# Two transformer blocks on one core: another order and another split of work in the attention pairs, and an output written in parts

## The reference

```python
# differential attention (4 head pairs): two softmaxes over the same values
p = softmax(q k^T * HD**-0.5)                  # one for each of the two maps
w = p[:, :, 0] - lam * p[:, :, 1]; out = w @ v # v is 128 wide
# windowed attention with sinks, neighbourhood attention, MLA: per head
out = softmax(q k^T * scale + bias) @ v        # v is 64 wide
# lam = exp(sum(lq1*lk1)) - exp(sum(lq2*lk2)) + lam_init
x = x + 0.5 * mx[8] * swiglu(...)              # the last layer's result is the output
```

## Time and profile before

| | |
|---|---|
| Median of 3 runs | 2604.9 us (2600.58 to 2605.96) |
| The profiled execution's own time | 2598.19 us |
| Its span | 2596.4 us |
| PE busy | 2490.1 us (96%), weight loads 2157.3 us (83%) |
| DVE busy | 1350.2 us (52%) |
| ACT busy | 1035.2 us (40%) |

### The profile page before, as it was taken

The page is one execution under the profiler, slowest core; times in us unless marked ns, Lnnn a source line. Parts: engine busy times, 40 slices in busy tenths (PEclk is TensorE's granted clock), DMA queues, the critical chain, the costliest instruction groups (busy, mean ns, idle before and its releaser), DMA issues.

```text
span 2596.4 us, 37247 instructions
## 1 busy us (share of the span) xinstructions
PE 2490.1 (96%) x15710; PEld 2157.3 (83%) x15710; DVE 1350.2 (52%) x2245; ACT 1035.2 (40%) x1659; POOL 0.2 (0%) x4
## 2 busy tenths in 40 slices
PE   7999999999999999999789999999999999988998
PEld 6998789978997888888568888888888887868998
DVE  6657554655453334357886333335333347846554
ACT  5534544434433223146563322213222226744442
POOL 0000000000000000000000000000000000000000
PEclk9999999999999999999999999999999999999999
DMA  9886733488862333335102323332333326502554
GB/s 334 283 277 207 234 122 98 145 321 302 311 211 90 97 98 98 97 122 186 41 1 66 103 96 96 96 97 90 97 97 97 98 89 181 184 1 67 185 180 137
DMA packets 145639, 372.28 MB, mean 143 GB/s; under 512 B 20266, under 2 KB 65730, under 8 KB 145474
## 3 DMA queue, kind: packets, MB, share of 16 engines
q1 hardware_dynamic: 145186, 369.59, 44.0%
q10 hardware_dynamic: 288, 0.31, 0.1%
HBM read 368.71 MB, written 1.15 MB: 142 GB/s over the span
## 4 chain that ended last, share of the span: by engine, by line
PE 88%; DVE 7%; ACT 3%; issue 1%; DMA 1%; SPq 0%; ACTq 0%; DVEq 0%
PE psum L352 76%; PE psum L834 2%; PE psum L1701 2%; PE psum L1672 1%; DVE normed_raw L618 1%; DVE normed_lo L631 1%; PE psum L1689 1%; PE psum L1603 1%; PE psum L1291 1%; PE psum L1303 1%; DVE weights_lo L300 1%; DVE arena L1768 0%; ACT arena L1721 0%; PE psum L1166 0%; PE psum L1275 0%
## 5 line engine op out<-in xcount | busy, mean ns | idle before, releaser
L300 DVE TENSOR_TENSOR weights_lo<-weights_raw,weights_hi 128x1024 fp32r<-128x1024 f32 (+2 forms) x547 | 656.9, 1212 | 471.8 <-ACT weights_hi L294 469.0
L352 PE MATMUL psum<-normed_hi,weights_hi 128*128 128x256 f32 (+2 forms) x2664 | 880.6, 331 | 21.6 <-DVE normed_lo L631 6.8
L352 PE MATMUL psum<-normed_lo,weights_hi 128*128 128x256 f32 (+2 forms) x2664 | 866.7, 325 | 0.0
L352 PE MATMUL psum<-normed_hi,weights_lo 128*128 128x256 f32 (+2 forms) x2664 | 866.3, 325 | 0.0
L294 ACT CAST weights_hi<-weights_raw 128x1024 fp32r<-128x1024 f32 (+2 forms) x547 | 562.8, 1035 | 371.8 <-DMA weights_raw<-in_w_down 260.9
L352 PEld LDWEIGHTS psum<-normed_hi,weights_hi 128*128 128x128 f32 (+1 forms) x2664 | 508.6, 191 | 85.5 <-issue 35.1
L352 PEld LDWEIGHTS psum<-normed_lo,weights_hi 128*128 128x128 f32 (+1 forms) x2664 | 509.8, 191 | 41.5 <-issue 1.2
L352 PEld LDWEIGHTS psum<-normed_hi,weights_lo 128*128 128x128 f32 (+1 forms) x2664 | 509.6, 191 | 40.6
L352 PE MATMUL psum<-hidden_hi,weights_hi 128*128 128x512 f32 (+1 forms) x594 | 217.6, 366 | 0.0
L352 PE MATMUL psum<-hidden_hi,weights_lo 128*128 128x512 f32 (+1 forms) x594 | 217.1, 365 | 0.0
L352 PE MATMUL psum<-hidden_lo,weights_hi 128*128 128x512 f32 (+1 forms) x594 | 217.1, 365 | 0.0
(11 more groups left out here) (264 smaller groups left out, 2740.3 us busy)
## 6 DMA issues: line engine op xcount, KB each, us to landing
weights_raw<-in_w_gu SPq DMA_DIRECT2D x220, 512.0 KB, 3.6
weights_raw<-in_w_down SPq DMA_DIRECT2D x110, 512.0 KB, 3.6
arena<-in_w_mod SPq DMA_DIRECT2D x72, 512.0 KB, 6.9
weights_raw<-in_w_x SPq DMA_DIRECT2D x24, 512.0 KB, 6.5
resid<-in_w_mod SPq DMA_DIRECT2D x24, 512.0 KB, 7.5
normed_raw<-in_w_mod SPq DMA_DIRECT2D x24, 512.0 KB, 7.9
under_normed_hi<-in_w_mod SPq DMA_DIRECT2D x24, 512.0 KB, 7.7
weights_raw<-in_w_qk SPq DMA_DIRECT2D x24, 512.0 KB, 4.3
```

The lines of the kernel that those rows point to most:

```text
L300: ve.tensor_tensor(w_lo[:, c % RING, a], w_raw[:, c % RING, a], w_hi[:, c % RING, a].bitcast(F32), ALU.subtract).then_inc(lo_ready, 1)
L352: last = te.matmul(out, a, b, start=start and n == 0, stop=stop and n == 2)
```

## The change

Five things change.

1. In `Attend`, PE now does the value products of unit i-3 ahead of the transposes of unit i-2. ACT copies banks 4 and 5 with one instruction; DVE's copy (L1735) and its semaphore go.
2. In a difference, L1779 goes. The second map's factor is formed as -lambda times the ratio of the sums, and one operation joins the maps; a second reciprocal comes behind it, and the output is scaled where it was copied. Other units scale both outputs with one operation instead of two.
3. In the second pass the side steps move: the second normalisation goes behind step 1, the eight turns behind steps 2 to 5.
4. `Modulation` waits for the constants only from its first transposes on.
5. The meetings of the engines, `Turn` and `Store` go. `Output` writes the result in five parts, woven into the last `IntoResid`, which no longer sums squares: four transposes each behind steps 7, 12 and 18 of its 22, and two transposes twice behind the last.

```diff
-                if 2 <= i < len(self.units) + 2:          # PE: transposes of unit i-2
-                    ...
                 if i >= 3:                                 # PE: values of unit i-3
                     j, u = i - 3, self.units[i - 3]
                     pe.wait_ge(aa_copied, self.base + j + 1)
-                    pe.wait_ge(*u.second)
                     ...
+                if 2 <= i < len(self.units) + 2:
+                    j, u = i - 2, self.units[i - 2]
+                    pe.wait_ge(*u.probs)
+                    if j >= 1:
+                        pe.wait_ge(aa_copied, self.base + j)
+                    ...
+                    last.then_inc(aa_turned, 1)
@@ Attend.scalar
-                    w = len(u.values[0]) * P
-                    se.copy(self.turned[:, j % 2, 0, 0:w], psum[:, 4, 0:w]).then_inc(aa_copied, 1)
+                    n, w = len(u.values), len(u.values[0]) * P
+                    se.copy(self.turned[:, j % 2, 0:n, 0:w], psum[:, 4:4 + n, 0:w]).then_inc(aa_copied, 1)
@@ Attend.vector
-                        ve.tensor_copy(self.turned[:, j % 2, 1, 0:w], psum[:, 5, 0:w]).then_inc(aa_copied2, 1)
...
+                    if u.lam is not None:
+                        last = ve.tensor_scalar(u.out, sums, stat[:, 2:3], None, ALU.mult)
+                    else:
+                        each = stat[:, 2:4].rearrange("p (n o) -> p n o", o=1).to_broadcast([P, 2, HD])
+                        last = ve.tensor_tensor(u.out, sums.rearrange("p (n d) -> p n d", n=2), each, ALU.mult)
@@ Attend.weights
-                step(ve.reciprocal(stat[:, 2:4], stat[:, 2:4]))
-                step(ve.tensor_tensor(stat[:, 3:4], stat[:, 3:4], u.lam, ALU.mult))
-                step(ve.tensor_scalar(s[:, 1, 0:u.width], s[:, 1, 0:u.width], stat[:, 3:4], None, ALU.mult))
+                step(ve.reciprocal(stat[:, 3:4], stat[:, 3:4]))
+                step(ve.scalar_tensor_tensor(out=stat[:, 3:4], in0=stat[:, 3:4], scalar=stat[:, 2:3], in1=u.lam,
+                                             op0=ALU.mult, op1=ALU.mult))
+                ve.scalar_tensor_tensor(out=s[:, 0, 0:u.width], in0=s[:, 1, 0:u.width], scalar=stat[:, 3:4],
+                                        in1=s[:, 0, 0:u.width], op0=ALU.mult, op1=ALU.add).then_inc(aa_probs, 1)
+                step(ve.reciprocal(stat[:, 2:3], stat[:, 2:3]))
@@ Modulation.tensor
                     pe.wait_ge(cond_in, 1)
+                elif k < 0:
                     pe.wait_ge(const_in, 32)
-                elif k < 0:
                     pe.wait_ge(mod_rows, r)
@@ second pass
-        side = [(0, h_steps[24]), (0, h_steps[25])]
-        side += [(1 + n // 2, t_steps[18 + n]) for n in range(8)]
+        side = [(0, h_steps[24]), (1, h_steps[25])]
+        side += [(2 + n // 2, t_steps[18 + n]) for n in range(8)]
@@ output
+            parts = ((0, 2), (2, 4), (4, 6), (6, 7), (7, 8))
+            def tensor(self, pe, i):
+                a, b = self.parts[i]
+                pe.wait_ge(*bank_free[self.down.group + b - 1])
+                for t in range(NT):
+                    for k in range(a, b):
+                        last = te.transpose(self.turned(i)[:, t, (k - a) * P:(k - a + 1) * P],
+                                            resid[:, k, t * P:(t + 1) * P], ident)
+                last.then_inc(out_mm, 1)
+            def scalar(self, act, step, i):
+                a, b = self.parts[i]
+                act.wait_ge(out_mm, i + 1)
+                se.copy(result[:, :, a * P:b * P], self.turned(i)).then_inc(out_copied, 1)
+            def sync(self, sp, i):
+                a, b = self.parts[i]
+                sp.wait_ge(out_copied, i + 1)
+                sp.dma_start(out[0].rearrange("(t p) n -> p t n", p=P)[:, :, a * P:b * P],
+                             result[:, :, a * P:b * P]).then_inc(out_done, 16)
...
-        alone(*chain, norm, *ffn(W["w_gu21"], W["w_down21"], KF, TOK, hidden_x, (1, 8), [norm]))
-        alone(Turn(...)); segments.append(([([Store()], 0, 1)], 0))
+        up, down = ffn(W["w_gu21"], W["w_down21"], KF, TOK, hidden_x, (1, 8), [norm], sums=False)
+        side = [((b * KF - 1) // CT + 2, step) for (_, b), step in zip(Output.parts, output)]
+        in_order(steps_of(*chain, norm, up), beside(steps_of(down), side))
```

More of the change, by code:

```diff
@@ L1680, in tensor @@
                     last.then_inc(aa_scores, 1)
-                if 2 <= i < len(self.units) + 2:
-                    j, u = i - 2, self.units[i - 2]
-                    pe.wait_ge(*u.probs)
-                    if j >= 1:
-                        pe.wait_ge(aa_copied, self.base + j)
-                        pe.wait_ge(*self.units[j - 1].second)
-                    for n in range(len(u.values)):
-                        for k in range(len(u.values[n])):
-                            last = te.transpose(psum[:, 4 + n, k * P:(k + 1) * P],
-                                                self.s[:, j % 3, n, k * P:(k + 1) * P], ident)
-                    last.then_inc(aa_turned, 1)
                 if i >= 3:
@@ L1704, in tensor @@
                     last.then_inc(aa_pv, 1)
+                if 2 <= i < len(self.units) + 2:
[3 more added lines that the diff above has]
+                        pe.wait_ge(aa_copied, self.base + j)
+                    for n in range(len(u.values)):
+                        for k in range(len(u.values[n])):
+                            last = te.transpose(psum[:, 4 + n, k * P:(k + 1) * P],
+                                                self.s[:, j % 3, n, k * P:(k + 1) * P], ident)
+                    last.then_inc(aa_turned, 1)
             def scalar(self, act, step, i):
@@ L1986, in ffn @@
+        def ffn(up, down, tiles, a, pair, gate, norms, tail=None, sums=True):
             first = FfnUp(up, tiles, a, pair, norms)
-            second = IntoResid(down, tiles, pair[1:], slice(0, a.stop - a.start), gate, tail=tail)
+            second = IntoResid(down, tiles, pair[1:], slice(0, a.stop - a.start), gate, sums=sums, tail=tail)
             second.ready = first.hidden_ready
@@ L2018, in build @@
         ctx_norm.have = lambda k: [(ctx_in, 16)]
-        segments.append(([
+        segments.append([
             ([attn_branch, mixer_out, norm2, *ffn0], 0, 1),
@@ L2023, in build @@
             ([Modulation(1, mod_ring1, (a1_max, NT * HG))], 0.1, 0.95),
-        ], 0))
+        ])
         last_norm = Norm(TOK, lambda k, s: col("final", k), None, into=resid)
-        def alone(*stages):
-            segments.append(([([stage], 0, 1) for stage in [Merged(steps_of(*stages))]], 1))
         def in_order(*lists):
-            segments.append(([([Merged([step for steps in lists for step in steps])], 0, 1)], 0))
+            segments.append([([Merged([step for steps in lists for step in steps])], 0, 1)])
         class Merged(Stage):
@@ L2256, in _ @@
         def _(pe):
-            for steps, n in plan:
+            for steps in plan:
                 for stage, i in steps:
                     stage.tensor(pe, i)
-                meet(pe, n)
         @block.scalar
```

119 lines of the change are left out of this document (34 added, 85 removed).

## The result

The changed kernel takes 2624.2 us (median of 5 runs, 2618.9 to 2627.4) where the kernel before takes 2603.8: a ratio of 1.0084, 95% interval 1.0072 to 1.0095, so 18.7 to 24.7 us more. I had put it at +6.4. Its profiled execution is the slowest of its runs (2627.4 us) and that of before a fast one (2598.2, where the runs go from 2597.8 to 2606.0), so their difference of 29.2 overstates the change: 10.4 of it stand ahead of the first pass, which begins at 1259.8 instead of 1249.4. Where it matters, the passes are therefore compared over several profiles.

What follows compares the result with a forecast made beforehand. PE was taken as the bound (88% of the path), with DVE pacing the first pass's first part. First pass 6.3 + second pass 2.9 - start 0.2 - end 2.6 = +6.4 on the median 2604.9: 2611.3 us, range 2598 to 2620.

Steps and rivals of the forecast that it cites:

- One such stretch more costs 0.6 here: First pass: after longer PE waits, one more stretch of matmuls runs at 1.2 instead of 2.4 GHz, +0.6 us.
- the low clock spreads: Rival: attention steps with idle time all run at half clock, up to +14 us, 2619; chance 0.07.
- Third, PE itself: First pass: value products wait for their unit's copy, 0.3 us exposed 4 times and 0.26 us 7 times, 3.0 us.
- First and second place (second turn, `SubNorm`): First pass, work queued on ACT behind copy and exponentials: step 8's evacuation 1.9 us later, `SubNorm` 2.3, three later tiles 3.9.
- DVE's relief: First pass differences: L1779 goes, a second reciprocal comes; 8 x 0.33 + 8 x 0.2 = 4.2 us gained.
- L1735's 1.2: First pass: gain from dropping DVE's copy, counted only at two early places where PE waits for it, 1.2 us.
- Second pass: Steps 0 to 6 take 41.6 us against 39.1, +2.4, and the last unit's copy adds 0.5: +2.9 in all.
- The start: First matmul could start 3.8 us earlier, but modulation chunks land at the same time: -0.2 us, -3.8 as other end.
- The end: Last matmul to end of span takes 5.1 us, not 9.15; twelve transposes among the products add 1.4: -2.6 us.
- DVE decides: Rival: DVE's relief of about 15.5 us in the first pass shortens it; 2590, or 2595 with half; chance 0.16.
- The two cancel: Rival: the low clock doesn't come and the exposed copies hide, -0.8 us, 2604; chance 0.13.
- the start comes through: Rival: earlier requests at the start fill gaps in the DMA engines, -3.6 us more, 2607.7; chance 0.09.

Runs made afterwards that it cites:

- e_start: Kernel before, with TensorE's wait for the constants moved from its first product to its first turn of modulation rows: -0.3 us (-2.9 to +2.3).
- e_end: Kernel before, with output transposes, copies and stores beside the last products in five parts, no engine meetings: -2.9 us (-4.9 to -0.5).
- e_side: Kernel before, with the second pass's second normalisation in step 1 and its turns in steps 2 to 5: -4.2 us (-6.5 to -1.8).
- e_order: Kernel before, with only TensorE's value products put ahead of the transposes of the unit behind them: 31.8 us slower (27 to 36).
- e_dve: Kernel before, with VectorE's part alone: one long operation less per difference, one scaling of both outputs: -3.1 us (-6.2 to -0.3).
- f_turns_first: Changed kernel with transposes ahead of value products again, all other edits kept: 2589.4 us, 12.0 below the kernel before (8.8 to 15.4).

## Why the prediction was wrong

**Sign right, size wrong.** Forecast +6.4, measured +21.9 (18.7 to 24.7). Over the profiles: first pass +16.4 (mean of the four profiles with the changed code, 134.2, against 117.8 of before, e_start, e_end and e_side), second pass some +8, end -3. They sum to 21.

**The step that failed: the clock in the first pass.** The text said "One such stretch more costs 0.6 here". Over the profiles with the same code (four with the changed code; before, e_start, e_end and e_side), TensorE's idle time in the first pass grew from 22.9 to 30.0 us, by 7.1, where the sum had 11.1 of new waits less 5.4 of relief, 5.7. Its busy time for the same instructions grew from 94.8 to 104.1, by 9.3, where the sum had 0.6. So of the 10.1 us that the first pass's forecast fell short, 8.7 are this one term. The waits' 1.9 + 2.3 + 3.9 + 3.0 = 11.1 also meet the idle time of the order alone (12.2 in the pair of profiles, 11.0 by the means); but the parts differ from mine, as the next paragraphs tell, so that agreement is in part luck. I had one stretch of low clock more; the order has TensorE wait in most steps, and behind many of these waits scores and products ran at 1.2 GHz (not behind all: after the 2.60 us in step 8 the scores took 1.13). For the second pass I had charged each new wait with 1.4 us of low clock, and that came out; I didn't carry it over to the first. The rival "the low clock spreads" named this, with a chance of 0.07 and a price of +14, and even that was short.

**"Third, PE itself" had the copy's wait right and left out a longer one.** The copy exposed 3.0 us as worked out, though in five waits and not in eleven. The longer wait was that for the output bank, 14.9 us (24.9 in e_order), which I never priced, because before it cost 2.9 in all. It stands where 10.9 us for the probabilities stood. An edit that moves an instruction ahead moves each of its waits ahead.

**First and second place (second turn, `SubNorm`): the path right, the first price half.** In step 8 the evacuation starts 6.22 us after the scores; the sum gave 7.22 with scores at the lower clock (2.01), and 6.27 with the 1.06 that they took. Before it was 5.32, so the delay is 0.9, not 1.9: here the low clock that I had charged didn't come. `SubNorm`'s square comes 6.22 us after step 9's scores, where 6.27 was forecast. VectorE's wait for it grew by 8.9 us over four tiles (0.5 before), for which I had 6.2; the order alone accounts for 7.3 of it. The Trainium skill (PSUM — Partial Sum Buffer, section "Engine vs sequencer instructions") has ScalarE's queue strictly first in, first out; the trace agrees, in that evacuation and square follow the exponentials of their step without a gap.

**DVE's relief: -4.2 forecast for the operations of e_dve, -3.1 (-6.2 to -0.3) measured.** Within its error. With L1735's 1.2 the forecast is -5.4; in the old order, with the single copy, the first pass is 5.1 shorter (f_turns_first), 4.7 by the means.

**Second pass: the steps right, the tail wrong.** From step 0 to step 6 I forecast 41.6 us; it took 41.8 (2294.06 to 2335.84), 39.1 before (so 2.5 more by my own figures, where I wrote 2.4), and its parts came out too: 11.6 to step 3, and three steps of 10.06 to 10.08 with the charge of 1.4 in each. Behind it step 6 took 1.6 more at the lower clock, and from the last scores to the end of the pass it took 18.3 us, not 15.7: each of the last units' products waits for its own copy (2.9 us in all), where I took 0.5. Together +6.7 on +2.9.

**The start: the landing right, the price missed.** The chunk's wait ended where I said, and the 3.8 us became waiting. That this wait can cost clock, and so put the kernel up to 3 us behind at 125 us, wasn't in the sum. By the runs the early start is worth 0 within 2.6 us.

**The end: -2.6 forecast, -2.9 alone (-4.9 to -0.5).** The tail is 3.9 us, not 5.1, mostly since from the last copy's end (2622.99) it takes 2.2 us, where issue, store and end were put at 3.3. The Trainium skill (DMA: Bandwidth & Descriptors, "Anatomy of one DMA") led to an estimate of 2.3 for the store alone. The 2.2 measured for issue, store and end together is below both, and nearer to that estimate than to my 2.8. That page's figure is for transfers that GpSimd's queue issues (the Trainium skill's own words are "SWDGE (gpsimd) path"), and this store is issued from SP's, so the nearness may be chance.

**Rivals.** "DVE decides" is refuted for this order. In the old one the whole gain is 12 us, as that rival had it, but not by its mechanism: the first pass is 5 us shorter, not 8 to 12, and the rest comes from the side steps (4.2 alone) and the end (2.9 alone). "The two cancel" and "the start comes through" are refuted.

**Open.** Which wait of the first pass leads is not settled: with the order kept, each of three cures (bank, exponentials, one step more of lag) moved waiting to another place or met a lower clock, and left the pass at 129 to 141 us. That the order costs it is shown in both directions; that VectorE's late squares, turns and scores are the core of it is read from two profiles, not isolated. That low clock costs time is shown by a fill in the second pass; for the first it is read from busy times.

## What to carry to other kernels

In a pipeline over several engines, an exchange of two blocks in one in-order queue is priced by the waits that it moves ahead, all of them, and by what stands behind the consumer on the next engine; removing the named wait can prove little, since it may come back under another name. Take a change of many parts apart: here five parts gained 10.5 us as the sum of their single runs (12.0 in one kernel), and the sixth lost 32. Where TensorE is the bound behind a wait, count the wait and then the products at half speed after it, or fill the wait.

## What the hardware showed that I had not expected

A wait of 2.65 us cost another 1.6 us in the scores behind it, and 18 transposes that compute nothing took this away (10.08 us a step to 8.37). Over both passes, nearly half of what the order added to TensorE's time was slower products. An earlier start made the program later at 125 us for the same reason: 3.6 us of lead became 3.4 us of waiting, and in ten of thirteen profiles a clock of 0.50 followed for 3.4 to 6.9 us. And where such stretches fall varies between executions of the same code: the first pass begins at 1247.7 to 1259.8 us over all the profiles, in no relation to the edits, which adds to the spread between the runs of one kernel (8.5 us in the changed one).
